# Hybrid attention layer on eight cores: engine of evacuations, squares, masks and scalings left to the scheduler

## What is computed

```
mod = silu(c) @ w_ada + b_ada; sh1, sc1, g1, sh2, sc2, g2 = split(mod)
h = rmsnorm(x, norm_mix_g) * (1 + sc1) + sh1
proj = h @ w_in
y_mla = mla_group(...)      # 8 heads, low-rank q and kv, rotary part, causal softmax
y_swa = swa_group(...)      # 8 heads, 2 kv heads, window 128, ALiBi, sinks
x = x + g1 * (concat(y_mla, y_swa) @ w_o)
h = rmsnorm(x, norm_mlp_g) * (1 + sc2) + sh2
u = square(relu(h @ w_up))
x = x + g2 * (u @ w_down)
return rmsnorm(x, final_g)
```

## Time and profile before

| what | us |
|---|---|
| median of three runs | 812.65 |
| the runs | 812.65, 874.0, 811.09 |
| time of the profiled execution | 812.65 |
| its span, on core 1, the slowest | 811.1 |
| TensorE busy | 742.4 (92%) |
| VectorE busy | 487.0 (60%) |
| ScalarE busy | 440.6 (54%) |
| GpSimd busy | 174.5 (22%) |

### The profile page before, as it was taken

How to read it: one execution, slowest core, us unless ns; L and a number is a source line. 1 busy time by engine, 2 the same in 40 slices (tenths; PEclk the granted TensorE clock), 3 DMA queues, 4 the chain that set the end, 5 groups by cost and what they waited for, 6 DMA issues and landing times.

```text
span 811.1 us, 15555 instructions; the slowest of 8 cores (798.6 to 811.1 us)
## 1 busy us (share of the span) xinstructions
PE 742.4 (92%) x5250; PEld 378.3 (47%) x5250; DVE 487.0 (60%) x851; ACT 440.6 (54%) x726; POOL 174.5 (22%) x156
## 2 busy tenths in 40 slices
PE   0679997999799999888979999999999999999996
PEld 0344555556456655544434444444444444444442
DVE  2386968635943444544765476754557576577757
ACT  3246645577688899983733522443234422445545
POOL 2020247576786433221040000000100000000000
PEclk9999999999999999999989999999999999999999
DMA  8999794699308683899961280330503331402115
GB/s 184 228 192 174 184 192 84 101 184 152 67 27 210 165 223 133 186 237 221 164 143 52 77 183 2 104 104 1 104 1 101 106 101 57 129 1 105 53 53 208
DMA packets 70397, 101.26 MB, mean 125 GB/s; under 512 B 39856, under 2 KB 47664, under 8 KB 70192
## 3 DMA queue, kind: packets, MB, share of 16 engines
q1 hardware_dynamic: 62112, 72.93, 33.5%
q0 software_dynamic: 8208, 27.33, 21.0%
HBM read 97.69 MB, written 20.71 MB: 146 GB/s over the span
## 4 chain that ended last, share of the span: by engine, by line
PE 80%; DMA 10%; issue 3%; DVE 3%; ACT 1%; POOL 1%; SPq 1%; DVEq 0%; ACTq 0%; POOLq 0%
PE ps L893 45%; PE ps L1739 23%; PE ps L1305 6%; PE ps L1329 3%; DMA arena<-winl 3%; DMA arena<-wup 3%; DMA arena<-wada 2%; PE ps L1351 2%; DMA arena<-x 1%; DMA arena<-mxs 1%; PE ps L1376 1%; DVE arena L1006 1%; PE ps L1190 0%; DVE arena L1702 0%; DVE arena L1153 0%
## 5 line engine op out<-in xcount | busy, mean ns | idle before, releaser
L893 PE MATMUL ps<-arena 128*128 128x512 bf16 (+2 forms) x2444 | 458.5, 332 | 41.3 <-DMA arena<-wada 24.7
L893 PEld LDWEIGHTS ps<-arena 128*128 128x128 bf16 x2444 | 197.6, 98 | 244.9 <-issue 57.8
L1702 DVE TENSOR_TENSOR arena<-ps,arena 128x512 f32<-128x512 f32 x194 | 129.3, 687 | 118.9 <-PE ps L1739 113.9
L1739 PE MATMUL ps<-arena 128*128 128x512 bf16 x840 | 188.3, 382 | 5.5 <-DVE arena L1700 5.5
L1551 ACT ACTIVATE arena<-ps 128x512 f32<-128x512 f32 x124 | 73.5, 596 | 197.3 <-PE ps L893 197.0
L1313 ACT ACTIVATE arena<-ps 128x1024 bf16<-128x1024 f32 (+1 forms) x160 | 137.9, 896 | 37.2 <-PE ps L1329 17.4
L1739 PEld LDWEIGHTS ps<-arena 128*128 128x128 bf16 x840 | 82.6, 98 | 106.4 <-issue 8.8
L1305 PE MATMUL ps<-arena 128*128 128x512 bf16 (+3 forms) x416 | 84.9, 305 | 3.2 <-ACT arena L1313 2.5
L964 ACT ACTIVATE arena<-arena 128x1024 bf16<-128x1024 f32 x47 | 49.6, 1054 | 67.0 <-DVE arena L1702 27.7
L1358 POOL TENSOR_TENSOR arena<-arena 128x1024 bf16<-128x1024 f32 x31 | 73.0, 2355 | 57.4 <-ACT arena L1355 34.3
L1553 ACT ACTIVATE arena<-arena 128x512 bf16<-128x512 f32 x124 | 77.5, 629 | 12.3 <-ACT arena L1551 1.1
(11 more groups left out here) (96 smaller groups left out, 445.6 us busy)
## 6 DMA issues: line engine op xcount, KB each, us to landing
arena<-x SPq DMA_DIRECT2D x32, 512.0 KB, 9.2
arena<-wdn SPq DMA_DIRECT2D x32, 512.0 KB, 4.3
arena<-wada POOLq DMA_DIRECT2D x24, 512.0 KB, 12.4
arena<-wup POOLq DMA_DIRECT2D x16, 512.0 KB, 11.2
out<-arena SPq DMA_DIRECT2D x15, 512.0 KB, 2.6
x1s<-arena SPq DMA_DIRECT2D x12, 512.0 KB, 3.6
arena<-x1s SPq DMA_DIRECT2D x12, 512.0 KB, 3.6
mxs<-arena SPq DMA_DIRECT2D x15, 256.0 KB, 4.7
```

Source lines behind the costliest of these rows:

```text
L893: S.op("pe", lambda h, i=i: h.matmul(out, lhsT=lhs_list[i], rhs=rhs_list[i], start=(i == 0), stop=(i == n - 1)), r=rbufs[i], w=[bankb[bank]])
L1702: S.op("dve", lambda h: h.tensor_tensor(out=X1[t][:, hs], in0=bk(b), in1=X1[t][:, hs], op=ALU.add), r=[bankb[b], bX1[t][half]], w=[bX1[t][ ...
L1739: S.op("pe", lambda h, f=f, av=av, wv=wv, p=p, b=b, first=first, n=n, key=key: h.matmul(bk(b), lhsT=av[:, f, p * 128:(p + 1) * 128], rhs=w ...
```

## The change

An operation may now have two forms, on two engines (`S.flex`). When it is ready, it stands in the queues of both, in that of the second form 500 ns later in planned time; the engine that comes to it first takes it, and the other skips it. These operations have two forms: the sums of squares (VectorE with an accumulator first, ScalarE second); evacuations of latents, swq, swk, keys and values (VectorE, ScalarE); triangle and window masks (GpSimd, VectorE); scaling of h2 (VectorE first; second GpSimd for groups 2 and 3, ScalarE for 0 and 1); relu (ScalarE, VectorE) and square (ScalarE, GpSimd) of the MLP. Besides, all four chunks of quarter q's up weights wait for what only chunk 0 waited for (with quarter 1, counted from 0, that is the load of h2 of group 2). The choice is made when the program is built; on the chip nothing is chosen. No operation is dropped.

```diff
+    def flex(self, fns, r=(), w=()):
+        first = next(iter(fns))
+        o = self.op(first, fns[first], r, w)
+        o.alts = fns
+        return o
...
+        if k.get("accum_out") is not None:
+            return 300.0 + 1.05 * n
...
         def release(o):
+            for i, e in enumerate(o.alts or (o.eng,)):
...
+                t += i * FLEX
+                if i == 0:
+                    o.rdy = t
+                heapq.heappush(fut[e], (t, o.pri, o.idx))
...
+            free[e] = t
...
+            if o.taken:
+                continue
+            if o.alts is not None:
+                o.eng = e
+                o.fn, o.dur, o.port = o.alts[e]
...
         def sumsq(src, bsrc, st, j, dst, bdst):
-            S.op("act", lambda h: h.activation(out=dst, in_=src, func=AF.Square, accum_out=STA[st][:, j:j + 1]),
-                 r=bsrc if type(bsrc) is list else [bsrc], w=[bSTA[st][j], bdst])
+            acc_ = STA[st][:, j:j + 1]
+            S.flex({"dve": lambda h: h.scalar_tensor_tensor(out=dst, in0=src, scalar=1.0, in1=src, op0=ALU.mult, op1=ALU.mult, accum_out=acc_),
+                    "act": lambda h: h.activation(out=dst, in_=src, func=AF.Square, accum_out=acc_)},
+                   r=bsrc if type(bsrc) is list else [bsrc], w=[bSTA[st][j], bdst])
...
+        def copy_out(dst, src, r, w, bias=None):
+            if bias is None:
+                S.flex({"dve": lambda h: h.tensor_copy(out=dst, in_=src), "act": lambda h: h.activation(out=dst, in_=src, func=AF.Copy)},
+                       r=r, w=w)
...
-            S.op("dve", lambda h: h.tensor_copy(out=LATS[G][m], in_=bk(b)), r=[bankb[b]], w=[bLATS[G][m]])
+            copy_out(LATS[G][m], bk(b), [bankb[b]], [bLATS[G][m]])
...
-                    S.op("pool", lambda h: h.tensor_tensor(out=v, in0=v, in1=TRI.unsqueeze(1).to_broadcast([128, m, 128]),
-                                                           op=ALU.mult), r=[bPT[p], bTRI], w=[bPT[p]])
+                    f = lambda h: h.tensor_tensor(out=v, in0=v, in1=TRI.unsqueeze(1).to_broadcast([128, m, 128]), op=ALU.mult)
+                    S.flex({"pool": f, "dve": f}, r=[bPT[p], bTRI], w=[bPT[p]])
...
-                if G == 0 or (G < 3 and k % 2):
-                    S.op("act", lambda h, hv=hv, g=g, m=m: h.activation(out=hv, in_=hv, func=AF.Identity, scale=g, bias=m), r=r, w=w)
-                else:
-                    S.op("pool" if G > 1 else "dve", lambda h, hv=hv, g=g, m=m: h.tensor_scalar(
-                        out=hv, in0=hv, scalar1=g, scalar2=m, op0=ALU.mult, op1=ALU.add), r=r, w=w)
+                S.flex({"dve": fv, "pool": fv} if G > 1 else {"dve": fv, "act": fa}, r=r, w=w)
...
-                      bWUP[s_][c], r=after if c == 0 else [], w=[bWUP[s_][c]])
+                      bWUP[s_][c], r=after, w=[bWUP[s_][c]])
```

More of the change, by code:

```diff
@@ L25 @@
 LAX = 6000.0
+FLEX = 500.0
 PARCOLS = []
@@ L105 @@
     __slots__ = ("eng", "fn", "deps", "sig", "cnt", "dma", "dbuf", "dval", "idx", "pri", "dur", "end", "nbytes", "start", "rdy", "why",
-                 "tens", "pk", "npk", "slack", "port")
+                 "tens", "pk", "npk", "slack", "port", "alts", "taken")
     def __init__(self, eng, fn):
@@ L121, in __init__ @@
         self.port = False
+        self.alts = None
+        self.taken = False
 class Probe:
@@ L262, in schedule @@
         for o in self.all:
-            o.dur = self.estimate(o)
+            if o.alts is not None:
+                for e, fn in o.alts.items():
+                    o.eng, o.fn = e, fn
+                    o.alts[e] = (fn, self.estimate(o), o.port)
+            else:
+                o.dur = self.estimate(o)
         tenants = {id(t): t for o in self.all for t in o.tens}
@@ L313, in release @@
         def release(o):
[L314 to L322, removed]
-                else:
[L324 to L328, removed]
+            for i, e in enumerate(o.alts or (o.eng,)):
+                t = 0.0
+                o.why = None
+                for (d, dv, kind) in o.deps:
+                    if kind in ("order", "fifo"):
+                        r_ = 0.0
+                    elif d.dma:
+                        r_ = d.end + o.slack
+                    elif d.eng == e:
+                        r_ = 0.0 if e in ("pe", "sp") else d.end + 100.0
+                    else:
+                        r_ = d.end + self.LAT[e]
+                    if r_ > t:
+                        t, o.why = r_, (d.eng, d.fn.__code__.co_firstlineno, kind)
+                t += i * FLEX
+                if i == 0:
+                    o.rdy = t
+                heapq.heappush(fut[e], (t, o.pri, o.idx))
         def place(o, t):
@@ L450, in schedule @@
                     for w in back:
-                        heapq.heappush(fut[w.eng], (max(w.rdy, min(bank_at[tn.i:tn.i + tn.width])), w.pri, w.idx))
+                        for e_ in w.alts or (w.eng,):
+                            heapq.heappush(fut[e_], (max(w.rdy, min(bank_at[tn.i:tn.i + tn.width])), w.pri, w.idx))
             if not o.dma:
@@ L1071, in a_swq @@
             src = bk(b).rearrange("p (a b) -> p a b", a=4, b=128)
[L1072 to L1077, removed]
+            copy_out(dst, src, [bankb[b], bBINR], [bSWQ[G % 2][c4]], BIN[:, 8 + c4:9 + c4])
         def a_swk(G):
@@ L1085, in a_swk @@
                     S.op("dve", lambda h, kv=kv: h.memset(SWK[G][64 - kv * 64:128 - kv * 64, kv, :], 0.0), w=[bSWKz[G]] if kv == 0 else [])
-                S.op("act", lambda h, kv=kv, rows=rows, rs=rs: h.activation(
-                    out=SWK[G % 3][rs, kv, :], in_=bk(b, rows), func=AF.Identity, bias=BIN[rs, 12:13]),
-                     r=[bankb[b], bBINR], w=[bSWK[G % 3][kv]])
+                copy_out(SWK[G % 3][rs, kv, :], bk(b, rows), [bankb[b], bBINR], [bSWK[G % 3][kv]], BIN[rs, 12:13])
         def a_swv(G):
@@ L1139, in a_k @@
                 src = bk(b, (half * 64, half * 64 + 64))
[L1140 to L1143, removed]
-                         r=[bankb[b]], w=[bKn[hh][G]])
+                copy_out(KG[G][0:64, hh, :], src, [bankb[b]], [bKn[hh][G]])
         def a_v(G, j):
```

31 lines of the change are left out of this document (15 added, 16 removed).

## The result

The changed kernel takes 791.98 us (median of four, 790.93 to 793.64) against 811.09 us (811.87 with the one execution of 874.0 us); the ratio is 0.9764, 95% interval 0.9735 to 0.9794. That is some 20 us, outside the 2%, inside the range of 786 to 818, and nearly twice the 11 us of the forecast. The time is that of rival (a), priced at 790 us; its parts are others, as shown further down.

The account below looks back on a forecast made before the run. TensorE, busy 92% of the span, was taken as the bound, gains lying in five stretches. Terms −5 −5 −2.5 +0 +1.5 = −11.0 gave span 800.1, plus 1.55: 801.6 us; 8-in-10 range 786 to 818.

Parts of the forecast that it names:

- rival (a): The port holds at 130 to 160 and 200 to 240 us go too: −11.7 more, 790 us; chance 0.20.
- Term 1: 410 to 440 us: moving h2 scalings off GpSimd ends a hold, 7.4 us, less 2.4 for VectorE's wait: −5.
- Term 2: 330 to 355 us: masks moved, window attention ends earlier, so the up weights no longer come 5 us late: −5.
- Term 3: 355 to 385 us: w_o input load of the last quarter starts earlier as attention ends earlier: −2.5 (−4 to 0).
- Term 4: 130 to 160 and 200 to 240 us: masks on VectorE, evacuations on ScalarE; between −11.7 and +6.6, taken as 0.
- (b): Around 200 to 260 us VectorE stands behind GpSimd; four holds cost 11 to 16 us, eight bring 828 us; chance 0.12.
- Term 5: 22 of 47 squares go to VectorE: +1 in the first 130 us, 0 in 260 to 390, +0.5 in the tail.
- the second slowest core: Other cores start 6.7 us or more ahead; with terms 2 and 3 of even half the size none ends later.

Follow-up runs that it names:

- the two scaling experiments: Scalings of h2 back on their old engines in the changed kernel: 799.21 us; scalings alone in two forms in the kernel before: 802.58 us.
- the last experiment: Changed kernel with no handicap for the second form (0 in place of 500 ns), 33 of 63 masks on VectorE: median span 786.8, largest 790.9 us.

## Why the prediction was half of it

*Term 1, scalings: −5 predicted, −7.4 came.* The mechanism was right, shown by the two scaling experiments. The 2.4 us set against it for VectorE's own wait were not paid on core 1. The wait did come, in VectorE's and TensorE's timeline of the changed kernel, core 1:

```profile
383.50 2.11 PE L921 MATMUL ps<-arena 128*128 128x512 bf16 x9
...
385.21 0.73 DVE L1474 TENSOR_SCALAR arena<-arena 128x512 bf16<-128x512 bf16 x2 [5.80 <-DMA arena<-arena]
...
390.89 2.68 DVE L1474 TENSOR_SCALAR arena<-arena 128x512 bf16<-128x512 bf16 x8 [0.20 <-issue]
```

VectorE stands 5.80 us for a tile transpose while TensorE streams up products, which ScalarE evacuates; the load of quarter 2's h2 had landed when VectorE came to it. On core 0, the slowest of that execution, the same wait was 8.86 us, and of these TensorE lost 1.49:

```profile
390.25 0.38 PE L1758 MATMUL ps<-arena 128*128 128x512 bf16 x1 [1.49 <-DVE arena L1541]
```

*Term 2, up weights: −5, came −5.2, in the main for another reason.* Of the 5.2 us that core 1 lost from 330 to 355 us before, 1.4 were the wait for up weights, as the earlier trace rows has it. The rest were waits for exponentials and for two triangle masks (TensorE's waits, core 1 before, 320 to 380 us):

```profile
PE ps L1305 <- ACT arena L1313: 1.7, 5, 0.7
PE ps L1329 <- POOL arena L1318: 1.6, 2, 0.8
```

These stood on all eight cores, the wait for up weights on cores 1 and 5 alone. So the load came 1.4 us late, not 5: the sum left out these 3.3 us, during which TensorE was not waiting for the weights. They ended with the change too, and are down to 1.3, 0.4 and 0.4 us with scalings, squares or masks alone (core 1 of each), so no one group is their cause. That the term came out right is luck. The first load is called for at 313.19 us, 15.4 us earlier than before. GpSimd's timeline:

```profile
313.19 0.59 POOL L1528 DMA_DIRECT2D arena<-wup  x1 [4.61 <-PE ps L1331]
314.91 1.66 POOL L1528 DMA_DIRECT2D arena<-wup  x3
```

The prediction gave this to the masks. Masks alone do it (317.27 us), squares alone (322.68) too, scalings alone not (331.20); either of the first two is enough.

*Term 3, w_o input: −2.5, came −4.0.* Both the wait and the low clock behind it went; before, two of the eight cores had that wait.

*Term 4, the two early stretches: 0, came −5.2.* This is the step that failed. It set 0 because the number of instructions that want the port from both sides is unchanged, so that new holds would cost what the old ones did. Before, both holds stood on all eight cores: 4.88 to 5.89 us at 135 us and 4.67 at 203, and TensorE waited for them. New ones did come, again on all eight cores, but shorter and with less waiting behind them. In the changed kernel, core 1:

```profile
141.09 4.46 DVE L1036 TENSOR_SCALAR arena<-arena 128x512 bf16<-128x512 bf16 x3
146.35 1.09 PE L921 MATMUL ps<-arena 128*128 128x1 bf16 x15 [1.84 <-DVE arena L1365]
...
203.94 2.94 DVE L1145 TENSOR_TENSOR arena<-arena 128x128 f32<-128x128 f32 x1
```

The first of the three scalings is held, 3.93 us, to the end of a row of masks, and TensorE waits 1.84 and 0.88 us behind it, where before it waited 3.9. Behind the rotation at 204 us it waits 0.3 us, where before it waited 2.7 (2.4 on core 4, where the rotation took 3.50). It is the masks that shorten these holds: with masks alone on two engines none of them is over 2.44 us, with the masks undone they are 5.6 and 3.2 to 3.8, with scalings alone 4.9 to 5.9 and 4.67, with evacuations alone 5.5 to 5.6 and 3.1 to 3.4. A mask costs GpSimd more than it costs VectorE:

```profile
L993 DVE SCALAR_TENSOR_TENSOR arena<-arena 128x1024 bf16<-128x1024 f32 x22 | 29.3, 1332 | 1.0 <-DVE arena L1497 0.2
...
L1773 DVE SCALAR_TENSOR_TENSOR arena<-arena 128x1024 f32<-128x1024 f32 x15 | 19.2, 1278 | 0.3 <-ACT arena L988 0.2
...
L1384 DVE TENSOR_TENSOR arena<-arena 128x1024 bf16<-128x1024 f32 x5 | 8.0, 1609 | 0.3 <-ACT arena L1381 0.3
...
L1344 DVE TENSOR_TENSOR arena<-arena 128x512 bf16<-128x512 bf16 x5 | 3.6, 727 | 0.0
...
L993 DVE DVE_READ_ACCUMULATOR arena<-arena 128x1 f32 x22 | 1.8, 82 | 0.0
```

Ten masks leave 17.6 us of GpSimd and take 8.0 + 3.6 = 11.6 on VectorE, one of the window masks being held (3.16 us). So GpSimd has less to do beside VectorE; that this is why the holds got shorter is the reading, not a test, and the last experiment, with 33 masks on VectorE and a longer hold at 200 us, speaks against it as a rule.

*The rivals.* (a) got the time and not the split: it priced the early stretches at −11.7, all that was lost there, while TensorE's waits for the two holds were 3.9 and 2.7 us. Of its 11.7 us 5.2 came, and the terms 1, 3 and 5 together brought 5.4 us more than the forecast had. That its 790 us came so near is luck. (b) was right that masks and rotations on VectorE would be held, and wrong on the price of 2.7 to 3.9 us each: besides the two above, instructions were held by 1 to 2 us at 200, 225, 291 and 299 us, and on core 1 TensorE waited 0.7 us at most behind any of these.

*Term 5, squares: +1.5, came about 0* (by the medians with and without, 788.3 and 789.0 us). They cost 1.332 + 0.082 us, near the row it was sized by. The Trainium skill's half rate for two f32 operands (Vector Engine (DVE) Microarchitecture Reference, "Points that are easy to get wrong") does not show with an accumulator either. The norms come later, TensorE's wait for them grows from 6.8 to 11.5 us, and its wait for the conditioning weights shrinks from 24.7 to 17.0: the transfer ends the stage in either case. With the squares back on ScalarE the two are 7.6 and 23.4.

*The other cores.* The prediction took the second slowest core, 6.7 us ahead, as a fixed distance and terms 2 and 3 at half. But the two early holds and most of what term 2 booked stood on every core; the hold at the first down product and the waits for up weights and w_o input differed from core to core: on one chip the spans of before had a median of 804.2 and a largest of 815.0. The median core gained 13 to 16 us and the spread the rest. Not all of the spread is from holds: at the rotations at 130 us the cores of before were 4.8 us apart already (127.72 to 132.50), those of the changed kernel 1.8 us at 141 us.

Not tried apart: triangle against window masks, relu and square of the MLP, the hold of quarter 2's up weights, and the length of a row of GpSimd instructions with all else the same.

## What to carry to other kernels

Where a VectorE instruction takes many times the mean of its like, look for GpSimd instructions back to back beside it, and look at all cores, before anything else; the sum of busy times does not show it. A hold that stands on all cores at the same place is paid by every core, and one that some cores have sets the slowest. The whole row is the upper bound of its price and one GpSimd instruction the lower; what counts in the end is the wait of the bounding engine behind it (here 2.7 us behind a hold of 3.93, and 0.3 behind one of 2.94). Before a stretch's idle time is booked as the gain of one cause, add up the list of waits in it: here the cause that was named had 1.4 of 5.2 us. A wait that is moved to another engine costs only if that engine evacuates what the bounding engine produces at that moment.

## What the runs showed of the hardware

A VectorE instruction from SBUF to SBUF that met a row of GpSimd instructions was held to the end of the row in some cases: 7.27 us of ten scalings before, 9.17 us for two sums beside 7.51 us with the scalings put back, 5.88 us for two scalings through three masks. In other cases it was through after at most one of them: 1.14 us on core 0 with the scalings put back, 1.22 to 1.62 us with masks alone. Then GpSimd waited as well: ten scalings took 8.43 us and not 7.51. The Trainium skill (SBUF — State Buffer, "Who interferes with whom") has the lock last for one instruction; the second kind agrees with it, and in the first the waiting engine did not get its turn between two.

Both kinds came under the same program in the same execution, at the first down product. At 135 and 203 us the hold stood on all eight cores, 4.88 to 5.89 us and 4.67 us.
